# The first tile's pair weights of both expert calls added into cleared DRAM tables by GpSimd, one-hot products for the other dense tiles

## The chip, the cores and the metric

The kernel runs on one core of a Trainium2 chip. Its time is the device time of one execution in microseconds (us). Differences are told against the median of three runs of the kernel before, 3693.56 us (3688.54 to 3696.64).

## The reference

Two transformer-like blocks follow each other over a sequence of 256 rows, with 256 more rows of context in the first layer. Most of the time goes into the expert layers ("PEER") of the first block, and they are all that the change touches. For each row h and each of 8 heads, 16 of 16384 experts are chosen; an expert number is a pair (i, j) of keys of 0 to 127 each:

```python
def _peer(h, wq, keys, u, v):
    q = (hb @ wq).reshape(tc, PEER_HEADS, 2, PEER_HALF)
    s = jnp.einsum('thpk,hpnk->thpn', q, keys)
    s_top, i_top = lax.top_k(s, PEER_TOPK)
    cand = s_top[:, :, 0, :, None] + s_top[:, :, 1, None, :]
    cid = i_top[:, :, 0, :, None] * N_KEYS + i_top[:, :, 1, None, :]
    best, pos = lax.top_k(cand.reshape(tc, PEER_HEADS, -1), PEER_TOPK)
    eid = jnp.take_along_axis(cid.reshape(tc, PEER_HEADS, -1), pos, -1)
    g = jax.nn.softmax(best, -1)
    act = jax.nn.gelu(jnp.einsum('td,thed->the', hb, u[eid]), approximate=False)
    return jnp.einsum('the,thed->td', g * act, v[eid])
```

D_MODEL is 1024, N_KEYS 128, PEER_HEADS 8, PEER_TOPK 16: each row has 128 chosen pairs (i, j) with a share g each. The first layer has four tiles of 128 rows (two of the sequence, two of the context), the second layer two.

## The kernel before

**How an expert layer is computed.** A dense tile doesn't gather its experts. It goes through all of them in two halves. The *score half* has 128 rounds, one per key: a round takes 128 experts' u rows (512 KB; SyncE loads two rounds' worth as a unit of 1 MB into `expert_ring`, 4 slots), splits them into a high part (ScalarE, `expert_high`) and a low part (VectorE, `expert_ring_low`), and multiplies them in 24 products with the tiles' rows in high and low parts; the gelu of the result goes to DRAM or is kept. The *v half* has 128 rounds as well: gelu times the *pair weights* of that key is split and multiplied with the v rows.

**Pair weights** are a table of 128 x 128 numbers for each row t: at (i, j) stands the sum of the shares of row t's chosen pairs (i, j), and zero elsewhere; for the v half they are wanted with i on the partitions. Which pairs are chosen is worked out during the score half itself, by VectorE (`select`, a generator: VectorE runs its pieces beside the ring's low parts, so much a round as a budget in nanoseconds allows). For each dense tile the selection, three columns per pair (i, j, share), is transposed by TensorE and copied to `pair_table`. The one-hot tables are then made in *table groups* of TOKS = 4 rows: VectorE compares `iota` with the table (`equal`, one instruction of 128x1024), ScalarE scales one of the two sides by the shares, TensorE makes one product per row (one-hot of i by weighted one-hot of j) into PSUM, ScalarE takes it out.

**First expert call** (`first_experts`, classes `ExpertsVector`, `ExpertsTensor`, `ExpertsScalar`, `ExpertsSync`, `ExpertsPool`). Its tiles are selected in the order TILES = (0, 3, 1, 2); 0, 1 and 2 are dense (DT = 3, DW = 384 columns), 3 is SPARSE. Table groups start in round TABLES_AT = 32: 96 groups, one a round, two in the twelve even rounds of 60 to 82 (`DOUBLED`). Blocks of 16 rows of the tables are staged and stored to `w_dram` by SyncE (`store_w`), and read back in the v half (24 blocks, `load_w`). The v half's rounds have 18 products each. The sparse tile's 128 pairs per row are handled one by one, as 128 *picks*: GpSimd gathers a u row for each partition by indirect DMA (into 3 slots, named `x` in rows of the profile, U_SLOTS = 3), VectorE multiplies it with the tile's rows and sums (line 3027), gelu follows for 8 picks at a time, GpSimd gathers the v row (`chosen_v`, V_SLOTS = 4) and VectorE adds it, weighted (line 3048). From the end of the selection on, these picks fill VectorE's budget. The budgets are EARLY_NS 3900, TABLE_NS 3300, PICKS_NS 2200 in three parts of the score half and DOWN_NS 1450 in the v half. Modulation products of a later stage are laid into some of the score rounds (`mod_slot`, 12 units).

**Second expert call** (`peer_experts` with PT = 2 tiles, W = 256 columns): selection on VectorE with a budget of SELECT_NS = 1650 a round, GROUPS = W / TOKS = 64 table groups, one in each round from TABLE_AT = 128 - 64 = 64 on; the tables stay in SBUF (`wt`, named `expert_weights`). There are no sparse picks, and GpSimd does nothing here.

**Order.** Each engine runs its instructions in program order. SyncE issues all plain loads and stores, in order; a load behind a wait in its queue waits too. GpSimd issues the indirect DMAs. The stage before the first expert call (`mixer`, lines about 1688 to 1693 on SyncE) loads `ab_w_in`, the scan mask, and two sets of weights (`in_w_mod`, `in_ab_w_out`) through `weight_ring`.

Lines that the rows below name: 2925 and 1922 the low parts of a round in the first and the second call, 3058 the comparison of a table group, 3178 and 2088 one of three sets of products of a round in the first and the second call (eight products a round each), 3217 the products of the first call's v half, 1897 a reduction of the second call's selection (the last piece but one of a tile), 3001 the shares of a tile in the first call's selection, 1176 the scan that reads the mask, 1305 the modulation product of the mixer stage.

## Time and profile before

| | us |
|---|---|
| median of three runs | 3693.56 (3688.54 to 3696.64) |
| the profiled execution, its own time | 3688.0 |
| its span in the trace | 3686.2 |
| TensorE busy | 3516.4 (95%) |
| VectorE busy | 2731.1 (74%) |
| ScalarE busy | 1690.3 (46%) |
| GpSimd busy | 348.6 (9%) |
| first call: score half | 485.7 to 1175.6 |
| first call: v half | 1183.2 to 1713.4 |
| second call: score half | 2012.9 to 2443.1 |

The profile has names of its own for the engines: PE is TensorE, with PEld its weight loads, DVE VectorE, ACT ScalarE, POOL GpSimd, SP SyncE, and SPq a DMA on SyncE's queue. A row of a timeline begins with the start and the duration in us, then engine, line, operation, output and input, and in brackets the engine's idle time before it and what ended that. A row of a group has the count behind the x, then busy time in us, mean in ns of one, and idle time before them. A row of a table by stretches has the stretch in us from the span's start, its length, the busy time of TensorE and of its weight loads with counts in brackets (of the named line alone, where one is named; of all five engines where none is), the granted clock of TensorE as a share of the full one, the share of time in which the DMA engines were busy, and GB/s moved.

### The profile page before, as it was taken

How to read it: one execution, taken by the hardware profiler on the slowest of the kernel's cores; microseconds unless marked ns; L12 is line 12 of the kernel's file. 1: busy time of each engine (PE TensorE's matmuls, PEld its weight loads, DVE VectorE, ACT ScalarE, POOL GpSimd, SP SyncE). 2: the span in 40 equal slices, each digit the busy share in tenths (PEclk: the TensorE clock that was granted, in tenths of full speed). 3: DMA queues.
4: the chain of work that ended last, by engine and by line, in shares of the span. 5: the costliest groups of instructions: out<-in, count | busy, mean ns of one | idle time of the engine just before them, and what ended most of it. 6: DMA issues, size and time to landing. Idle time of an engine off the chain costs nothing. (4 is left out here: it accounts for less than half of the span.)

```text
span 3686.2 us, 56123 instructions
## 1 busy us (share of the span) xinstructions
PE 3516.4 (95%) x21807; PEld 3143.1 (85%) x21807; DVE 2731.1 (74%) x5467; ACT 1690.3 (46%) x3033; POOL 348.6 (9%) x274
## 2 busy tenths in 40 slices
PE   7999999989999999998999999999997899989899
PEld 6777998989998888887778999988886889988798
DVE  4557379988885888887546987778887677767775
ACT  4343333556663333334543444443334545564554
POOL 0000000014443333330000000000000000000000
PEclk9999999999999999999999999999998999999999
DMA  5133357569998999995124765556664214432143
GB/s 229 71 115 137 138 194 300 173 224 340 371 375 296 333 391 370 377 357 186 56 86 156 233 220 172 169 197 243 242 245 165 98 63 169 186 142 109 69 183 137
DMA packets 184072, 766.75 MB, mean 208 GB/s; under 512 B 23360, under 2 KB 70976, under 8 KB 133888
## 3 DMA queue, kind: packets, MB, share of 16 engines
q1 hardware_dynamic: 146944, 628.92, 47.3%
q0 software_dynamic: 36864, 134.23, 9.4%
q8 instruction: 175, 2.87, 0.3%
q14 instruction: 89, 0.73, 0.1%
HBM read 696.24 MB, written 66.85 MB: 207 GB/s over the span
## 5 line engine op out<-in xcount | busy, mean ns | idle before, releaser
L2925 DVE TENSOR_TENSOR expert_ring_low<-expert_ring,expert_high 128x1024 fp32r<-128x1024 f32 x256 | 312.9, 1222 | 143.5 <-ACT expert_high L3283 137.2
L3283 ACT ACTIVATE expert_high<-expert_ring 128x1024 fp32r<-128x1024 f32 x256 | 270.6, 1057 | 276.2 <-PE ps L3217 264.0
L2192 ACT ACTIVATE expert_high<-expert_ring 128x1024 fp32r<-128x1024 f32 x256 | 270.6, 1057 | 211.3 <-PE ps L2119 211.3
L1922 DVE TENSOR_TENSOR expert_ring_low<-expert_ring,expert_high 128x1024 fp32r<-128x1024 f32 x256 | 311.6, 1219 | 70.7 <-ACT expert_high L2192 70.7
L3178 PE MATMUL ps<-hidden_high,expert_high 128*128 128x384 f32 x1024 | 352.6, 344 | 0.0
L3179 PE MATMUL ps<-hidden_low,expert_high 128*128 128x384 f32 x1024 | 344.4, 336 | 0.0
L3180 PE MATMUL ps<-hidden_high,expert_ring_low 128*128 128x384 f32 x1024 | 344.0, 336 | 0.0
L2088 PE MATMUL ps<-peer_hT_high_peer,expert_high 128*128 128x256 f32 x1024 | 293.9, 287 | 0.6 <-DVE expert_ring_low L1922 0.5
L2089 PE MATMUL ps<-peer_hT_low,expert_high 128*128 128x256 f32 x1024 | 287.0, 280 | 0.0
L2090 PE MATMUL ps<-peer_hT_high_peer,expert_ring_low 128*128 128x256 f32 x1024 | 287.0, 280 | 0.0
L3484 POOL DMA_INDIRECT x<-in_peer_rows,spots x128 | 171.1, 1336 | 971.0 <-ACT mod_next L2378 558.8
L3217 PE MATMUL ps<-expert_high,weighted_high 128*128 128x512 f32 x768 | 237.7, 391 | 9.4 <-DVE weighted_low L3098 9.4
L3217 PE MATMUL ps<-expert_ring_low,weighted_high 128*128 128x512 f32 x768 | 237.0, 390 | 0.0
L3217 PE MATMUL ps<-expert_high,weighted_low 128*128 128x512 f32 x768 | 237.0, 390 | 0.0
L5596 PE MATMUL ps<-hT_high,units_high 128*128 128x256 f32 x704 | 200.2, 284 | 0.0
L5596 PE MATMUL ps<-hT_low,units_high 128*128 128x256 f32 x704 | 199.5, 283 | 0.0
L5596 PE MATMUL ps<-hT_high,weight_ring_low 128*128 128x256 f32 x704 | 199.4, 283 | 0.0
L3490 POOL DMA_INDIRECT chosen_v<-in_peer_v,spots x128 | 171.1, 1336 | 263.2 <-DVE x L3048 246.9
L2088 PEld LDWEIGHTS ps<-peer_hT_high_peer,expert_high 128*128 128x128 f32 x1024 | 194.4, 190 | 1.2 <-DVE expert_ring_low L1922 1.2
L219 DVE TENSOR_TENSOR weight_ring_low<-weight_ring,units_high 128x1024 fp32r<-128x1024 f32 (+1 forms) x148 | 166.9, 1189 | 38.3 <-ACT units_high L210 38.1
L3178 PEld LDWEIGHTS ps<-hidden_high,expert_high 128*128 128x128 f32 x1024 | 194.1, 190 | 0.8 <-issue 0.8
L2089 PEld LDWEIGHTS ps<-peer_hT_low,expert_high 128*128 128x128 f32 x1024 | 194.7, 190 | 0.0
(790 smaller groups left out, 9616.4 us busy)
## 6 DMA issues: line engine op xcount, KB each, us to landing
expert_ring<-in_peer_u SPq DMA_DIRECT2D x128, 1024.0 KB
expert_ring<-in_peer_v SPq DMA_DIRECT2D x128, 1024.0 KB
weight_ring<-in_ffn_w_up SPq DMA_DIRECT2D x22, 2048.0 KB, 7.3
weight_ring<-in_w_in SPq DMA_DIRECT2D x14, 2048.0 KB, 7.8
weight_ring<-in_w_mod SPq DMA_DIRECT2D x12, 2048.0 KB, 8.6
mod_slot<-in_w_mod SPq DMA_DIRECT2D x12, 2048.0 KB, 10.4
pair_weights<-pair_weights_out SPq DMA_DIRECT2D x24, 1024.0 KB
pair_weights_in<-pair_weights SPq DMA_DIRECT2D x15, 1536.0 KB, 15.6
```

What stands on the lines that cost most here:

```text
L1922: dve.tensor_tensor(piece(low, n), piece(raw, n), high[:, n % LEAD, :].bitcast(F32), ALU.subtract).then_inc(low_done, 1)
L2088: pe.matmul(o, b[:, s], hT_h[:, c, :], start=(c == 0), stop=False)
L2089: pe.matmul(o, b[:, s], hT_l[:, c, :], start=False, stop=False)
L2090: mm = pe.matmul(o, lo[:, s], hT_h[:, c, :], start=False, stop=(c == DC - 1))
L2192: act.activation(high[:, n % LEAD, :], piece(raw, n), ACT.Identity).then_inc(high_done, 1)
L2925: dve.tensor_tensor(self.piece(G.e_low, n), self.piece(G.e_raw, n), G.e_high[:, n % LEAD, :].bitcast(F32), ALU.subtract).then_inc(self.S.l ...
L3178: pe.matmul(o, b[:, s], B.hs[0][:, c, 0:DW], start=(c == 0), stop=False)
L3179: pe.matmul(o, b[:, s], B.hs[1][:, c, 0:DW], start=False, stop=False)
L3180: mm = pe.matmul(o, lo[:, s], B.hs[0][:, c, 0:DW], start=False, stop=(c == DC - 1))
L3217: mm = pe.matmul(G.ps[:, 2 * t + h, :], (B.ah, B.al)[x][:, r % 3, t * P:(t + 1) * P], v[y][:, h * 512:(h + 1) * 512], start=(r == 0 and (x ...
L3283: act.activation(G.e_high[:, n % LEAD, :], self.piece(G.e_raw, n), ACT.Identity).then_inc(S.high_done, 1)
L5596: mm = pe.matmul(G.ps[:, k % 8, 0:SEQ], w[x][:, c, q * P:(q + 1) * P], self.hT[y][:, c, :], start=(c == 0 and (x, y) == PASSES[0]), stop=( ...
```

## The change

*In both expert calls tile 0 (STREWN) leaves the one-hot path.* Its pair weights are made in DRAM: two areas, 8 blocks of `w_dram` (`pair_weights`) for the first call and `late_pairs` (`late_pair_weights`) for the second, are cleared in the mixer stage by 16 DMAs of 1 MB each from a constant of zeros. VectorE works out, for each partition (row) and pair, the place in that area (`own_spots`, `spots`), and GpSimd issues 128 indirect DMAs a call, each of which adds 128 shares, one per partition, to their places (`strew`; every sixteenth waits for all before it to land). The transposition and the table groups of that tile go: 64 groups are left in the first call, from round 48 (TABLES_AT) to 111, one each, and 32 in the second, from round 96. In the first call 96 strews stand ahead of the sparse tile's gathers on GpSimd, the other 32 between them. The second call loads tile 0's weights from `late_pairs` to SBUF in 9 DMAs, three in the score half and six in the v half. VectorE's budgets in the first call become 3200, 3000, 2300 and 1500.

```diff
@@ mixer stage, SyncE
                     ws.run_ahead(sp, u0 + 6)
+                    for b in range(OWN_BLOCKS):
+                        sp.dma_start(G.w_dram[b], G.d["zeros"]).then_inc(G.cleared, 16)
+                    for k in range(0, P, 2 * P // CLEARS):
+                        sp.dma_start(G.late_pairs[k:k + 2 * P // CLEARS, :].rearrange("i (p n) -> (i p) n", n=2 * D), G.d["zeros"]).then_inc(
+                            G.cleared, 16)
@@ peer_experts
-GROUPS = W // TOKS
+GROUPS = (W - P) // TOKS
+CLEARS = 16
+    LOADS = [(N_KEYS - KEPT, KEPT), (0, 12)] + [(k, 16) for k in range(12, N_KEYS - KEPT, 16)]
@@ peer_experts, VectorE
+                    if t == 0:
+                        step(dve.scalar_tensor_tensor(where[:, :], sel[:, t, 0, :], float(N_KEYS), sel[:, t, 1, :], ALU.mult,
+                                                      ALU.add))
...
+                    if t == 0:
+                        dve.wait_ge(base_landed, 16)
+                        dve.tensor_scalar(spots[:, :], where[:, :], float(P), base[:, 0:1], ALU.mult, ALU.add).then_inc(own_ready, 1)
@@ peer_experts, GpSimd
+        @block.gpsimd
+        def _(pool):
+            places = G.late_pairs.rearrange("i (n o) -> (i n) o", o=1)
+            pool.wait_ge(G.cleared, 16 * CLEARS)
+            pool.wait_ge(own_ready, 2)
+            for m in range(PAIRS):
+                if m and m % PEER_TOPK == 0:
+                    pool.wait_ge(G.strewn, 16 * (PAIRS + m))
+                pool.indirect_dma_start(places, bass.IndirectOffsetOnAxis(spots[:, m:m + 1], 0), shares[:, m:m + 1], None,
+                                        compute_op=ALU.add).then_inc(G.strewn, 16)
@@ peer_experts, SyncE
+            def load_pairs(n):
+                first, size = LOADS[n]
+                by_key = G.late_pairs.rearrange("i (j t) -> i j t", t=P)
+                sp.dma_start(wt[:, first:first + size, 0:P], by_key[:, first:first + size, :]).then_inc(pairs_landed[n], 16)
...
+                if p == UNITS_U - 3:
+                    sp.wait_ge(table_ready, 1)
+                    if mod is not None:
+                        sp.wait_ge(mod_out, 1)
+                    sp.wait_ge(G.strewn, 2 * 16 * PAIRS)
+                    for n in range(3):
+                        load_pairs(n)
...
+                if q % 8 == 0 and 3 + q // 8 < len(LOADS):
+                    load_pairs(3 + q // 8)
@@ first call
-TABLES_AT = 32
-TABLES = DW // TOKS
+TABLES_AT = 48
+TABLES = (DW - P) // TOKS
-EARLY_NS, TABLE_NS, PICKS_NS, DOWN_NS = 3900, 3300, 2200, 1450
+EARLY_NS, TABLE_NS, PICKS_NS, DOWN_NS = 3200, 3000, 2300, 1500
-DOUBLED = range(60, 84, 2)
-TABLE_ROUND = [r for r in range(TABLES_AT, N_KEYS) for _ in range(2 if r in DOUBLED else 1)][0:TABLES]
+STREWN = 0
+STREWN_FIRST = 6 * PEER_TOPK
+OWN_BLOCKS = P // BLOCK
+TABLE_ROUND = range(TABLES_AT, TABLES_AT + TABLES)
@@ first call, SyncE, before the loads for the v half
-                sp.wait_ge(S.table_ready, DT)
+                sp.wait_ge(S.table_ready, DT - 1)
+                sp.wait_ge(G.strewn, 16 * PAIRS)
@@ first call, GpSimd
+    def strew(self, pool, m):
+        G, B = self.G, self.B
+        places = G.w_dram.rearrange("b p (n o) -> (b p n) o", o=1)
+        if m and m % PEER_TOPK == 0:
+            pool.wait_ge(G.strewn, 16 * m)
+        pool.indirect_dma_start(places, bass.IndirectOffsetOnAxis(B.own_spots[:, m:m + 1], 0), B.own_share[:, m:m + 1],
+                                None, compute_op=ALU.add).then_inc(G.strewn, 16)
 
     def run(self, pool):
         G, S, B = self.G, self.S, self.B
+        pool.wait_ge(G.cleared, 16 * CLEARS)
+        pool.wait_ge(S.own_ready, 2)
+        for m in range(STREWN_FIRST):
+            self.strew(pool, m)
         pool.wait_ge(S.spots_ready, 1)
...
+            if STREWN_FIRST + n < PAIRS:
+                self.strew(pool, STREWN_FIRST + n)
```

**What stands on SyncE in the mixer stage**, between the last loads of `ab_w_in` and the two sets of weights that follow the mask; lines with + are new, lines with - are gone (the mask's load has another line number now).

```order
 L1688 DMA probs<-in_ab_norm_w 128x512
 L172 DMA weight_ring<-in_ab_w_in 128x4096 x3
-L1693 DMA scan_mask<-in_scan_mask 128x2560
+L1691 DMA pair_weights<-in_zeros 16x16384 x8
+L1693 DMA late_pair_weights<-in_zeros 16x16384 x8
+L1698 DMA scan_mask<-in_scan_mask 128x2560
 L172 DMA weight_ring<-in_w_mod 128x4096 x8
 L172 DMA weight_ring<-in_ab_w_out 128x4096 x2
```

Sixteen copies from DRAM to DRAM now stand ahead of the mask and of the weights behind it.

**What stands on GpSimd at the start of the first expert call**, before: `x` are the slots of the gathered u rows, `spots` the places of the sparse tile.

```order
L3601 UNCONDITIONAL_BRANCH
L3484 DMA x<-in_peer_rows,spots_4913 128x1024 x10
L3490 DMA chosen_v_4882<-in_peer_v,spots_4913 128x1024
L3484 DMA x<-in_peer_rows,spots_4913 128x1024
L3490 DMA chosen_v_4882<-in_peer_v,spots_4913 128x1024
```

And of the change, the last strews of the 96 and the first gathers: `big_21`, `big_44` and `big_34` are the waits for the sparse tile's places, for the last modulation unit and for the first table; `shares_strewn` counts strews that have landed.

```order
L3535 DMA pair_weights<-own_shares_4929,own_spots_4928 6291456x1 [waits shares_strewn]
L3535 DMA pair_weights<-own_shares_4929,own_spots_4928 6291456x1 x15
L3551 DMA x<-in_peer_rows,spots_4931 128x1024 [waits big_21,big_44,big_34]
L3535 DMA pair_weights<-own_shares_4929,own_spots_4928 6291456x1 [waits shares_strewn]
L3551 DMA x<-in_peer_rows,spots_4931 128x1024
L3535 DMA pair_weights<-own_shares_4929,own_spots_4928 6291456x1
```

The gathers that were first on GpSimd now stand behind 96 strews, and the first 32 of them have a strew between any two.

**What stands on SyncE where the second call goes from its score half to its v half**, before: `gelu_peer` is the store of a round's results, `big_15` the wait for the last table product.

```order
L2297 DMA gelu_peer<-gelu_out 128x512 [waits big_3]
L2280 DMA expert_ring<-in_peer_v 128x2048 [waits big_2] x2
L2287 DMA gelu_in_peer_20369<-gelu_peer 128x1024 [waits big_5,big_4] x2
L2308 DMA x<-x_spill 128x2048 [waits big_15]
L2280 DMA expert_ring<-in_peer_v 128x2048 [waits big_20] x4
```

And of the change:

```order
L2329 DMA gelu_peer<-gelu_out 128x512 [waits big_3]
L2311 DMA expert_weights<-late_pair_weights 128x4x128 [waits shares_strewn,big_13]
L2311 DMA expert_weights<-late_pair_weights 128x12x128
L2311 DMA expert_weights<-late_pair_weights 128x16x128
L2306 DMA expert_ring<-in_peer_v 128x2048 [waits big_2] x2
L2318 DMA gelu_in_peer_19921<-gelu_peer 128x1024 [waits big_5,big_4] x2
L2348 DMA x<-x_spill 128x2048 [waits shares_strewn,big_15]
L2306 DMA expert_ring<-in_peer_v 128x2048 [waits big_20]
```

Three loads of tile 0's weights, behind a wait for all strews, now stand ahead of the last two units of v rows (unit 66 and 67) that the score half loads.

## Rows read from the trace of the kernel before

**Rows 1.** The page's span, and its busy time by engine.

```profile
span 3686.2 us, 56123 instructions
PE 3516.4 (95%) x21807; PEld 3143.1 (85%) x21807; DVE 2731.1 (74%) x5467; ACT 1690.3 (46%) x3033; POOL 348.6 (9%) x274
```

**Rows 2.** Table by stretches, first call's score half, line 3178 alone.

```profile
485.70:654.50 168.80, 84.26 (x248) 46.58 (x248) 1.00 0.72 266
654.50:799.30 144.80, 72.50 (x209) 39.92 (x209) 0.98 0.53 179
799.30:826.80 27.50, 11.01 (x33) 6.05 (x33) 0.91 0.87 311
826.80:974.00 147.20, 70.08 (x201) 38.41 (x201) 0.98 0.94 343
974.00:1125.60 151.60, 82.66 (x241) 45.19 (x241) 1.00 0.98 375
1125.60:1175.60 50.00, 32.13 (x96) 17.97 (x96) 1.00 0.82 315
```

**Rows 3.** The same for the second call's score half, line 2088 alone.

```profile
2012.90:2178.60 165.70, 130.91 (x464) 88.02 (x465) 1.00 0.69 223
...
2204.60:2443.10 238.50, 142.39 (x489) 92.69 (x489) 1.00 0.52 171
```

**Rows 4.** Groups of VectorE in the first call's score half.

```profile
L2925 DVE TENSOR_TENSOR expert_ring_low<-expert_ring,expert_high 128x1024 fp32r<-128x1024 f32 x127 | 155.0, 1220 | 87.6 <-ACT expert_high L3283 82.8 <-issue 4.5
L3058 DVE TENSOR_TENSOR equal<-iota,pair_table 128x1024 f32<-128x1024 f32 x96 | 115.8, 1218 | 0.0
```

**Rows 5.** VectorE's timeline at four places.

```profile
493.64 1.23 DVE L2925 TENSOR_TENSOR expert_ring_low<-expert_ring,expert_high 128x1024 fp32r<-128x1024 f32 x1 [7.85 <-ACT expert_high L3283]
...
558.40 0.29 DVE L3001 TENSOR_TENSOR selected<-best_exp,best_sum 128x128 f32<-128x128 f32 x1
...
794.04 1.21 DVE L3027 SCALAR_TENSOR_TENSOR x<-x,hidden_rows 128x1024 f32<-128x1024 f32 x1
...
2091.72 2.27 DVE L1897 TENSOR_REDUCE selected<-one_hot 128x128 f32<-128x2048 f32 x1
```

**Rows 6.** Table by stretches, first call's v half, line 3217 alone.

```profile
1183.20:1713.40 530.20, 525.20 (x2304) 433.43 (x2304) 1.00 0.95 348
```

**Rows 7.** Timelines of GpSimd and VectorE around the first call's gathers.

```profile
657.35 1.39 POOL L3484 DMA_INDIRECT x<-in_peer_rows,spots  x1 [0.30 <-issue]
659.05 0.94 POOL L3484 DMA_INDIRECT x<-in_peer_rows,spots  x1 [0.30 <-issue]
...
803.89 1.89 POOL L3484 DMA_INDIRECT x<-in_peer_rows,spots  x1 [1.74 <-DVE x L3027]
...
816.65 1.22 DVE L3027 SCALAR_TENSOR_TENSOR x<-x,hidden_rows 128x1024 f32<-128x1024 f32 x1 [4.07 <-DMA x<-in_peer_rows,spots]
```

**Rows 8.** Groups of GpSimd, whole span.

```profile
L3484 POOL DMA_INDIRECT x<-in_peer_rows,spots x128 | 171.1, 1336 | 971.0 <-ACT mod_next L2378 558.8 <-DVE x L3027 400.2 <-issue 11.9
```

**Rows 9.** SyncE's timeline in the mixer stage.

```profile
112.11 0.33 SPq L172 DMA_DIRECT2D weight_ring<-in_ab_w_in  x1
115.16 0.33 SPq L1693 DMA_DIRECT2D scan_mask<-in_scan_mask  x1
152.68 133.08 SPq L172 DMA_DIRECT2D weight_ring<-in_w_mod  x8
```

**Rows 10.** Table by stretches, mixer stage, all engines.

```profile
112.00:153.00 41.00, 41.00 (x197) 28.97 (x195) 22.79 (x53) 17.43 (x36) 0.00 (x0) 1.00 0.21 84
153.00:196.00 43.00, 43.00 (x215) 30.57 (x215) 23.65 (x59) 18.20 (x42) 0.00 (x0) 1.00 0.13 50
```

**Rows 11.** Lines 1176 and 1305: ns min/median/max, first and last start.

```profile
L1176 DVE SCALAR_TENSOR_TENSOR mlstm_d<-ps,gcol,scan_mask x32: 475/617/753, 244.8 to 305.5; 128x256 f32<-128x256 f32 x16, 128x512 f32<-128x512 f32 x16
...
L1305 PE MATMUL ps<-weight_ring,silu_c x128: 592/592/617, 250.0 to 307.4; 128*32 128x512 f32 x128
```

**Rows 12.** The page's DMA issues: KB each, us from issue to landing.

```profile
pair_weights_in<-pair_weights SPq DMA_DIRECT2D x15, 1536.0 KB, 15.6
```

More of the change, by code:

```diff
@@ L97, in stage @@
         loads_landed = own[-1]
-        assert len(names) + (3 if beside is not None else 0) < len(own)
+        assert len(names) + (3 if beside is not None else 0) + (1 if loads else 0) <= len(own)
         @block.sync
@@ L1785, in peer_experts @@
         mod.slots = arena.take("mod_slots", [P, 2, UNIT], F32)
-    table, hot_i, hot_j, ge_in, aw, ah, al = small
+    spots, shares, base, table, hot_i, hot_j, ge_in, aw, ah, al = small
+    where = arena.take("spot_sums", [P, PAIRS], F32)
+    LOADS = [(N_KEYS - KEPT, KEPT), (0, 12)] + [(k, 16) for k in range(12, N_KEYS - KEPT, 16)]
     if end.cols:
@@ L1910, in select @@
+                    dve.tensor_tensor(share.rearrange("p (h m) -> p h m", h=PEER_HEADS), ex[:, t, :, :],
+                                      sm[:, t, :, 1:2].broadcast_to([P, PEER_HEADS, 16]), ALU.mult).then_inc((own_ready, sel_ready)[t], 1)
                     yield 300
-                for t in range(PT):
-                    at[f"turn{t}"] = at["now"] + TURN_AFTER
-                    yield (TURN_AFTER + 1) * SELECT_NS
-                    dve.wait_ge(sel_turned, t + 1)
-                    dve.tensor_copy(table[:, :, t * P:(t + 1) * P],
-                                    ps[:, 3, 0:3 * P].rearrange("p (k c) -> p k c", k=3)).then_inc(table_ready, 1)
-                    yield 600
@@ L1918, in select @@
-                assert at[f"turn{PT - 1}"] < TABLE_AT
+                at["turn"] = at["now"] + TURN_AFTER
+                yield (TURN_AFTER + 1) * SELECT_NS
+                dve.wait_ge(sel_turned, 1)
+                dve.tensor_copy(table[:, :, :], ps[:, 3, 0:3 * P].rearrange("p (k c) -> p k c", k=3)).then_inc(table_ready, 1)
+                yield 600
+                assert at["turn"] < TABLE_AT
             def split_low(n):
@@ L1940, in weigh @@
                     dve.wait_ge(ge_landed[m % 2], 16 * (m // 2 + 1))
+                for n, (first, size) in enumerate(LOADS):
+                    if expert(r) == first:
+                        dve.wait_ge(pairs_landed[n], 16)
                 if r >= 1:
@@ L2144, in _ @@
                     pe.wait_ge(score_s, SCORES // 2)
-                for t in range(PT):
-                    if r == at[f"turn{t}"]:
-                        turn_selected(t)
+                if r == at["turn"]:
+                    turn_selected()
                 u = mod_unit(r)
@@ L2216, in _ @@
                 split_high(r + LEAD)
-                if r == at["shift"]:
-                    for t in range(PT):
+                for t in range(PT):
+                    if r == at[f"shift{t}"]:
                         act.wait_ge(shift_ready, t + 1)
@@ L2997, in select @@
                 dve.tensor_copy(B.spots[:, :], B.where[:, :]).then_inc(S.spots_ready, 1)
+            elif tile == STREWN:
+                dve.wait_ge(S.base_landed, 16)
+                dve.tensor_scalar(B.own_spots[:, :], B.where[:, :], float(BLOCK), B.base[:, 0:1], ALU.mult,
+                                  ALU.add).then_inc(S.own_ready, 1)
             yield 600
             step.wait()
-            share = (B.share[:, :] if tile == SPARSE else sel[:, 2, :]).rearrange("p (h m) -> p h m", h=PEER_HEADS)
+            share = {SPARSE: B.share[:, :], STREWN: B.own_share[:, :]}.get(tile, sel[:, 2, :]).rearrange("p (h m) -> p h m", h=PEER_HEADS)
             mm = dve.tensor_tensor(share, B.ex[:, :, :], B.sm[:, :, 1:2].broadcast_to([P, PEER_HEADS, 16]), ALU.mult)
@@ L3003, in select @@
                 step(mm)
+                yield 300
+                continue
+            if tile == STREWN:
+                mm.then_inc(S.own_ready, 1)
                 yield 300
@@ L3184, in turn_selected @@
         G, S, B = self.G, self.S, self.B
-        k = [n for n, t in enumerate(TILES) if t != SPARSE][d]
+        k = [n for n, t in enumerate(TILES) if t not in (SPARSE, STREWN)][d]
         pe.wait_ge(S.sel_ready, d + 1)
@@ L3250, in run @@
                 pe.wait_ge(S.score_s, SCORE_GROUPS // 2)
-            for d in range(DT):
+            for d in range(DT - 1):
                 if r == at[f"turn{d}"]:
@@ L3421, in run @@
                     mod.load(sp, u + 2, self.mod_landed)
-            while stored < BLOCKS and TABLE_ROUND[4 * stored + 3] + 2 <= UJ * p + 1:
+            while stored < BLOCKS - OWN_BLOCKS and TABLE_ROUND[4 * stored + 3] + 2 <= UJ * p + 1:
                 self.store_w(sp, stored)
@@ L3582, in first_experts @@
     F.ln_cols = few.take("ln_cols", [P, 2, DC], F32)
+    B.base = few.take("own_base", [P, 1], F32)
     B.x_last = F.x_last = room(28.25, 4).take("x_last", [P, D], F32)
```

73 lines of the change are left out of this document (42 added, 31 removed).

## The prediction

> **What bounds the kernel now.** The page comes first: TensorE is busy 95% of a span of 3686.2 us [rows 1]. Its ends are modelled, so the share alone proves nothing; the rounds have to be timed. I cut both score halves (one round for each of 128 keys i) into stretches and counted rounds as eighths of the matmul records of one line [rows 2, 3].
>
> In the first call the 31 rounds from 485.7 take 168.8 us, 5.45 each; the next 26 take 144.8, 5.57 each; then 4 rounds take 27.5 and 25 take 147.2; the next 30 take 151.6, 5.05 each; the last 12 take 50.0, 4.17 each [rows 2]. The last ones hold no table group, the 30 before them one group each: 4.17 is TensorE's own pace for 24 products, and a table group (4 one-hot products) adds 0.88. In the second call 58 rounds without a group take 165.7 us, 2.86 each, and 61 of the 64 rounds with one take 238.5, 3.91 each: a group costs 1.05 [rows 3].
>
> Why the first call's rounds 31 to 56 are slower than 4.17 + 0.88 is read from VectorE. Each round it makes the low part of a key's rows and, from round 31, one comparison for a group; both are rows of 1.22 us [rows 4], and the rest of the round is selection. Selection runs from 493.64 to the first pick of the sparse tile at 794.04 [rows 5], 300.4 us with little idle time between. So the first call is VectorE's up to about round 57, and TensorE's behind it.
>
> The v halves are TensorE's: 2304 products in 530.2 us, at a DMA share of 0.95 [rows 6]. The change leaves their products alone.
>
> **Removed.** *Second call.* Tile 0 no longer passes through the table, so 32 of the 64 group rounds become plain: 32 x (3.91 - 2.86) = **33.6 us** on TensorE, whose rounds are back to back. VectorE needs 1.22 + 1.65 us in a plain round by its budget, which is the 2.86 measured, so selection hides as before.
>
> *First call*, in three pieces.
> (a) Rounds 0 to 30 hold no groups. TensorE's products, the modulation parts and kept rows set 168.8 us; VectorE's budget falls from 3.9 to 3.2 us a round, which nobody waits for here. Gain 0 (to 5).
> (b) Rounds 31 to 60 took 144.8 + 27.5 = 172.3 us. After, 13 of them hold a group: 30 x 4.17 + 13 x 0.88 = 136.5 us for TensorE. VectorE's check: selection now spreads over 61 of its rounds instead of 54 (+7 low parts of 1.2) with 16 comparisons in them instead of 25 (-9 x 1.2), so its work is some 298 us at most; rounds 0 to 60 last 168.8 + 136.5 = 305. It fits with little to spare; I take 138. Gain 34.
> (c) Rounds 61 to 115 took 147.2 + 151.6 = 298.8 us, twelve of them with two groups. After, rounds 61 to 111 hold one group and 112 to 115 none: 51 x 5.05 + 4 x 4.17 = 274.2. Gain 25. The last 12 stay at 50.0.
>
> The four rounds from 799.3 hold a stall that only moves: 27.5 - 4 x 5.05 = 7.3 us, where VectorE's first picks wait for rows [rows 2]. A gather issued at 803.89 is used at 816.65 [rows 7], 10.9 us after its issue ended. The next picks come in pairs per round while GpSimd now has a strew between any two gathers, so I charge 10 us for it after (7 to 16).
> First call: 34 + 25 - 10 = **49 us** gained.
>
> **Added, and what hides it.** *Strews.* A strew is an accumulating scatter of 128 four-byte words from GpSimd. None is in the trace. The nearest row is its indirect gather of 128 rows: 1.336 us mean, 0.30 us between two that wait for nothing [rows 7, 8], 1.64 us apiece. Below, 0.94 + 0.30 (the shortest shown); above, twice the work of a gather, as an add must read its target before it writes: 2 x 1.336 + 0.30 = 2.97. I take 1.64, the row itself. Every sixteenth waits for all before it to land: between 0 and 10.9 us; I take 4.
>
> First call: tile 0 is selected by round 14, so about 485.7 + 15 x 5.45 = 567, ready near 569 (before, at 558.4 [rows 5]). 96 strews: 157 us, 5 waits 20: GpSimd is free at **746**. Its first gathers must have landed for the first pick, behind round 61: 654.5 + 138 + 5 = about 798. Spare 50 us; the chain shows once a strew costs more than (798 - 569 - 20) / 96 = 2.18 us. The other 32 ride between picks: u, v and strew are 4.9 us of GpSimd, against a pick every 5.05 / 0.9 = 5.6 us. In this order the sparse gathers queue behind the strews on GpSimd, and VectorE, then TensorE, behind the gathers.
>
> Second call: tile 0's last reduction starts at 2091.72 [rows 5], ready near 2095. 128 strews 210 us, 7 waits 28: done at **2333**. SyncE waits for them behind round 123, at 2012.9 + 96 x 2.86 + 28 x 3.91 = 2397; what is queued behind that wait is every later load of expert rows. Spare 64 us; threshold 2.15 us a strew.
>
> *The rule that speaks against it.* GpSimd's row is of a gather that only copies [rows 8]. The Trainium skill (Collectives: The Full Stack, "The bandwidth ceiling: the fold count and why AG ≠ RS ≠ AR") says that a DMA which adds needs two source reads, so two read descriptors for each piece, and gets half a copy's rate. No run here shows one. By the rule the sum would be the first rival's, 3796; by the row it is 3614.
>
> *Clears.* 16 DMAs of 1 MB, DRAM to DRAM, on SyncE between the load at 112.11 and that of the mask at 115.16 [rows 9]. The core moves 84 GB/s in 112 to 153 and 50 in 153 to 196 [rows 10]; the mask is first read at 244.8, the weights loaded from 152.68 on at 250.0 [rows 9, 11]. What waits in SyncE's queue behind them is the mask and those weights, and VectorE's scan waits for the mask. 16.8 MB in 112.4 to 244.8, less 5 us for the mask, needs 132 GB/s. The trace has no DRAM-to-DRAM copy. Traffic ran at up to 375 GB/s [rows 2]; I take half of it as an estimate, since each byte is read from and written to DRAM: 188 GB/s, 90 us, over at 203. Cost 1 (0 to 5), issue included.
>
> *Pair loads of the second call.* Three of 2 MB together, in 512-byte pieces, go ahead of unit 66. The first call's load of the same pieces lands 1.5 MB in 15.6 us [rows 12]; 2 MB then take 21, and the first two (1 MB), which VectorE needs first, 10.4 of the 15.6 us of rounds 124 to 127. Unit 66 lands near 2422, needed near 2425. Cost 3 (0 to 8). The six later ones ride in a v half far from full.
>
> VectorE's share of v rounds grows by 50 ns of budget in 4.14 us. Nothing.
>
> **Sum**, against the profiled 3688.0: - 49 - 33.6 + 1 + 3 = -79, 3609. The median of the three runs is 5.6 above that execution, so 3693.6 - 79 = 3615; I say **3614**.
>
> **Rivals.**
> *1. A strew costs about twice a gather, and the result is slower.* At 2.97 us: first call 96 x (2.97 - 2.18) = 76 us before the first pick, second call 128 x (2.97 - 2.15) = 105 us of SyncE's wait. 3694 - 79 + 181 = **3796**. For it: the add's second read, and a landing of 10.9 us under load. Against: GpSimd's gathers vary from 0.94 to 1.89 us at one size [rows 7], so its time is not the bytes, and there are 128 words as there were rows. It decides from 2.52 us a strew on (224 c = 79 + 96 x 2.18 + 128 x 2.15). Chance 0.13.
> *2. The same, milder*: 2.2 to 2.5 us, at 2.35 a delay of 16 + 26: **3657**, still faster. 0.09.
> *3. VectorE stays the bound in the first call*, because selection in rounds 31 to 60 keeps its 5.57 us: 30 x 5.57 = 167, piece (b) gives 5 instead of 34: **3643**. Against it: its sum of work above. 0.08.
> *4. The clears are slow.* At 100 GB/s they end at 280 and the mask comes 40 us late: **3655**; at 81 GB/s they eat the gain. 0.03, and a third of that beyond.
> *Forecast* 0.67.
> In the first call's rounds 61 to 111 DMA is at a share of 0.98 and 375 GB/s [rows 2]; picks come 4.5% denser. If 375 were a wall, 0.04 MB more in 1.9 MB a round costs 51 x 0.11 + 2 = 8 us. It is in the range, not a rival.
>
> **Range.** The forecast's own bounds: (a) -5, stall -3 to +6, clears to +4, loads -3 to +5, DMA wall +8, DVE in (b) +6: 3600 to 3643, and to 3590 for what shorter strews and idle time might give. Rivals 3, 2 and half of 4 reach 3660. Low 3586, high 3662 leaves out rival 1 and some of the edges. A change within 0.2% (7 us) can't be told from none here: faster 0.85, same 0.02, slower 0.13.
>
> **What would show it.** In the trace after: second call, 96 rounds at 2.86 then 32 at 3.91, and no idle of TensorE from 2390 on for pair weights; first call, the first sparse pick at about 800 with GpSimd idle since 746; rounds with one group at 5.05; scan mask read without a wait for DMA. Wrong if a strew's row is above 2.1 us, if TensorE idles for a gather at the first pick, if the first v round of the second call starts more than 10 us after the last score round, or if the rounds 31 to 60 take over 150 us.

## The result, and the profile after

The changed kernel takes 3654.03 us (median of four runs, 3653.88 to 3655.86) against 3693.48 before: a ratio of 0.9896, 95% interval 0.9878 to 0.9913. It is faster by 39 us (32 to 45), where 79 were forecast: inside the stated range of times, but with a little under half of the forecast gain. Its profiled execution took 3654.15 us. Of the runs further down, two of the four executions of `plain_writes` and one of `strews_spread` fell in a slower state and are left out of their medians.

The page of the changed kernel, span and busy time by engine, as in [rows 1]:

```profile
span 3652.4 us, 54815 instructions
PE 3460.5 (95%) x21289; PEld 3086.7 (85%) x21289; DVE 2639.5 (72%) x5181; ACT 1623.9 (44%) x2843; POOL 830.3 (23%) x530
```

TensorE is busy 56 us less, the span is 34 us shorter: 22 us of new idle time have to be found. The stages, as in [rows 2, 3] (columns as there; line 3231 is a set of products of the first call's score rounds, 2105 of the second's):

```profile
489.50:658.00 168.50, 84.24 (x248) 46.55 (x249) 1.00 0.79 266
658.00:806.00 148.00, 82.38 (x241) 45.86 (x241) 0.98 0.62 161
806.00:1106.80 300.80, 152.88 (x441) 84.16 (x441) 0.98 0.97 351
...
1995.70:2273.00 277.30, 217.03 (x769) 145.85 (x769) 1.00 0.76 223
2278.00:2399.60 121.60, 72.33 (x248) 47.05 (x248) 1.00 0.64 154
```

The first three are the first call's rounds 0 to 30, 31 to 60 and 61 to 115: 168.8, 172.3 and 298.8 us before [rows 2]. The third was to fall to 284 and rose by 2. The last two are the second call's rounds 0 to 95 and 97 to 127.

The groups of GpSimd in the changed kernel (3535 the first call's *strews*, the indirect DMAs that add the shares; 2299 the second's; 3551 and 3557 the gathers of u and v rows):

```profile
L2299 POOL DMA_INDIRECT late_pair_weights<-pair_shares,pair_spots x128 | 246.8, 1928 | 488.5 <-DVE pair_shares L1924 412.9 <-issue 48.5 <-DMA late_pair_weights<-pair_shares,pair_spots 27.1
L3535 POOL DMA_INDIRECT pair_weights<-own_shares,own_spots x128 | 241.2, 1885 | 538.1 <-DVE own_shares L3050 473.6 <-issue 43.0 <-DMA pair_weights<-own_shares,own_spots 21.6
L3557 POOL DMA_INDIRECT chosen_v<-in_peer_v,spots x128 | 171.3, 1338 | 210.7 <-DVE x L3101 190.7 <-issue 20.1
L3551 POOL DMA_INDIRECT x<-in_peer_rows,spots x128 | 164.5, 1285 | 243.5 <-DVE x L3080 229.2 <-issue 14.3
```

A strew takes 1.885 and 1.928 us; with the idle time put down to issue (43.0 / 128 and 48.5 / 128) it is 2.22 us in the first call and 2.31 in the second, where the prediction took the gather's 1.64. The waits for landing, at seven places a call, are 21.6 / 7 = 3.1 and 27.1 / 7 = 3.9 us each; 4 was taken.

What that does in the first call, on GpSimd's and VectorE's timelines: the last of the 96 strews and the first gather, then a later stretch.

```profile
805.50 1.64 POOL L3535 DMA_INDIRECT pair_weights<-own_shares,own_spots  x1 [0.30 <-issue]
807.45 1.04 POOL L3551 DMA_INDIRECT x<-in_peer_rows,spots  x1 [0.30 <-issue]
808.87 2.46 POOL L3535 DMA_INDIRECT pair_weights<-own_shares,own_spots  x1 [0.38 <-issue]
...
843.33 1.23 DVE L3080 SCALAR_TENSOR_TENSOR x<-x,hidden_rows 128x1024 f32<-128x1024 f32 x1 [8.14 <-DMA x<-in_peer_rows,spots]
...
873.11 0.98 POOL L3551 DMA_INDIRECT x<-in_peer_rows,spots  x1 [0.31 <-issue]
874.39 1.76 POOL L3557 DMA_INDIRECT chosen_v<-in_peer_v,spots  x1 [0.30 <-issue]
876.45 1.61 POOL L3535 DMA_INDIRECT pair_weights<-own_shares,own_spots  x1 [0.30 <-issue]
878.37 1.33 POOL L3551 DMA_INDIRECT x<-in_peer_rows,spots  x1 [0.30 <-issue]
...
882.18 1.23 DVE L3080 SCALAR_TENSOR_TENSOR x<-x,hidden_rows 128x1024 f32<-128x1024 f32 x1 [3.34 <-DMA x<-in_peer_rows,spots]
```

GpSimd gets to its first gather at 807, not at 746. From there to the last strew its gaps are 0.3 us but for six (0.38 to 2.58 us, 9 us together): it is all but full while the strews ride between the gathers, and VectorE waits for rows, up to 8.14 us at a time. A table by stretches shows it for all engines (fifth pair: GpSimd):

```profile
848.00:976.00 128.00, 116.24 (x693) 114.38 (x694) 100.44 (x112) 70.99 (x164) 104.60 (x68) 0.95 0.96 332
976.00:1106.80 130.80, 130.80 (x822) 130.80 (x822) 114.59 (x125) 75.23 (x168) 70.52 (x50) 1.00 1.00 388
```

In the first stretch GpSimd issues 68 transfers in 128 us: 104.6 us of work and 67 gaps of at least 0.3 us leave some 3 us. TensorE idles 11.8 us there. The last strew goes out at 974; behind it TensorE has no idle time.

In the second call, SyncE and VectorE between the two halves:

```profile
2384.51 0.39 SPq L2329 DMA_DIRECT2D gelu_peer<-gelu_out  x1
2407.11 2.13 SPq L2311 DMA_DIRECT2D expert_weights<-late_pair_weights  x3
...
2410.33 0.42 DVE L1961 TENSOR_TENSOR weighted<-gelu_out,expert_weights 128x256 f32<-128x256 f32 x1 [10.18 <-DMA expert_weights<-late_pair_weights]
...
2411.59 1.22 PE L2134 MATMUL ps<-expert_high,weighted_high 128*128 128x512 f32 x2 [10.91 <-DVE weighted_low L1969]
```

The first strew of this call goes out at 2083.2 and the last ends at 2405.6: 322 us for the 128, where 238 were forecast. SyncE has waited 22 us for it, and TensorE 10.91 us.

And the clears, which cost nothing:

```profile
115.98 0.33 SPq L172 DMA_DIRECT2D weight_ring<-in_ab_w_in  x1
116.35 5.11 SPq L1691 DMA_DIRECT2D pair_weights<-in_zeros  x8
121.50 5.02 SPq L1693 DMA_DIRECT2D late_pair_weights<-in_zeros  x8
126.64 0.50 SPq L1698 DMA_DIRECT2D scan_mask<-in_scan_mask  x1
156.55 133.08 SPq L172 DMA_DIRECT2D weight_ring<-in_w_mod  x8
```

From the load ahead of them to the next weights it is 40.57 us, as before (112.11 to 152.68, [rows 9]). The 3.9 us by which all of this is late arise ahead of the clears, and at the first score product the changed kernel is still 3.8 us late (489.50 against 485.70), so nothing behind the clears waited for them. In the 41 us from 116 the core moves 355 GB/s against 84 before, in the next 43 us 181 against 50: that is 16.7 MB more, so by this table the 16.8 MB of zeros were over by about 200 at the latest, as forecast (203).

### The profile page after: what moved, and what is told of

It reads as the page before. It is cut to its first block and busy times, and to the rows that moved or that the text cites. A ratio compares the mean times of both kernels' runs of the same rounds, so it can differ in the third digit from the quotient of the medians.

```text
span 3652.4 us, 54815 instructions
## 1 busy us (share of the span) xinstructions
PE 3460.5 (95%) x21289; PEld 3086.7 (85%) x21289; DVE 2639.5 (72%) x5181; ACT 1623.9 (44%) x2843; POOL 830.3 (23%) x530
## 5 line engine op out<-in xcount | busy, mean ns | idle before, releaser
L3535 POOL DMA_INDIRECT pair_weights<-own_shares,own_spots x128 | 241.2, 1885 | 538.1 <-DVE own_shares L3050 473.6
L2299 POOL DMA_INDIRECT late_pair_weights<-pair_shares,pair_spots x128 | 246.8, 1928 | 488.5 <-DVE pair_shares L1924 412.9
```

## The experiments

Stages in us, each read from its own trace (first call's rounds 0 to 30, 31 to 60, 61 to 115; second call's rounds 0 to 95; from the last product of line 2105 in the second call to its first v product) and the median of the runs. The changed kernel's own two traces differ by 2.6 us in the rounds 61 to 115 and by 3.6 in the gap, so smaller differences than that say nothing. The profiled execution of `no_strews_1` was the fastest of its four (3626.0), that of `no_strews_2` the slowest (3656.3). The kernel before ran beside them at 3690.1, 3691.0 and 3691.5.

| kernel | 0-30 | 31-60 | 61-115 | second 0-95 | to v | median |
|---|---|---|---|---|---|---|
| before | 168.8 | 172.3 | 298.8 | 308.9 | 3.3 | 3693.5 |
| changed | 168.5 | 148.0 | 300.8 | 277.3 | 12.3 | 3654.0 |
| changed_again | 168.5 | 148.0 | 303.4 | 277.3 | 8.7 | 3655.4 |
| no_strews_1 | 168.5 | 147.9 | 281.3 | 277.3 | 8.2 | 3637.1 |
| no_strews_2 | 168.5 | 148.0 | 306.0 | 277.2 | 3.4 | 3647.1 |
| plain_writes | 284.0 | 146.6 | 288.7 | 337.6 | 3.4 | 3808.5 |
| gathers_ahead | 168.5 | 148.0 | 303.9 | 277.3 | 12.1 | 3656.2 |
| strews_spread | 168.5 | 148.0 | 287.7 | 277.3 | 8.4 | 3639.0 |
| budgets | 177.9 | 142.5 | 300.2 | 277.3 | 12.3 | 3655.8 |
| spread_and_budgets | 177.9 | 142.5 | 293.9 | 277.3 | 12.2 | 3652.9 |
| units_first | 168.5 | 147.9 | 303.7 | 277.3 | 9.9 | 3655.7 |
| second_call_only | 168.8 | 169.9 | 301.4 | 277.3 | 12.4 | 3672.5 |
| all_three | 168.5 | 148.0 | 284.1 | 277.3 | 12.2 | 3635.6 |

**No strews in the first call.** The other hunks only lower the counts that are waited for. Tile 0's pair weights of that call stay zero.

```diff
-        for m in range(STREWN_FIRST):
-            self.strew(pool, m)
...
-            if STREWN_FIRST + n < PAIRS:
-                self.strew(pool, STREWN_FIRST + n)
```

> The changed kernel without the 128 strews of the first call (left out: tile 0's pair weights of the first call, which stay zero); clears, budgets and table rounds as in the changed kernel. Theory G (GpSimd's strews, 2.2 us each and 2.4 with their waits, hold back the sparse gathers): the rounds 61 to 115 of the first score half come down from 300.8 us to about 282 (274 and the old stall of 7), and the whole to about 3636. Rival V (VectorE's own work, picks beside table groups, holds these rounds): no change, 3651 to 3656. By both the rounds 31 to 60 stay at about 148, since no gather is in them.

Measured 3637.07 us (ratio to before 0.986, 0.9844 to 0.9877), rounds 61 to 115 at 281.3 us, rounds 31 to 60 unchanged. Theory G holds in size, and V falls. Its groups of waits, VectorE between 795 and 1110 us:

```profile
DVE expert_ring_low L2972 <- ACT expert_high L3336: 27.0, 38, 2.0
DVE x L3080 <- DMA x<-in_peer_rows,spots: 13.0, 6, 5.6
```

In the changed kernel the second of these is 28.9 us with 8.6 more in two gaps put down to issue. This run also shows what the late first gather costs: here it goes out at 720, and VectorE's first pick still starts at 812.4, against 814.6 in the changed kernel, whose first score product is as much later (489.5 against 487.4). The end of the selection sets the first pick, not the gather; only from the second on, with its 6.51 us, does VectorE wait for rows in the changed kernel.

**No strews in the second call.** The counts waited for are lowered here too. Tile 0's pair weights of that call stay zero.

```diff
-            for m in range(PAIRS):
-                ...
-                pool.indirect_dma_start(places, bass.IndirectOffsetOnAxis(spots[:, m:m + 1], 0), shares[:, m:m + 1], None,
-                                        compute_op=ALU.add).then_inc(G.strewn, 16)
```

> The changed kernel without the 128 strews of the second call (left out: tile 0's pair weights of the second call, which stay zero); the pair loads stay. Theory G: SyncE's wait for the strews (22 us) goes, the gap of TensorE between score half and v half of the second call falls from 11.0 us to 2 to 4, and the whole to about 3643. Rival L (the three pair loads ahead of the last v units cost it, whenever they are issued): the gap stays near 11, the whole at 3651 to 3656.

The gap falls to 3.4 us, that of before (3.3). 3647.12 us (0.9879, 0.9862 to 0.9896). G holds: the strews' end is what TensorE waited for, the pair loads are not. The median falls by 6.9 us, the gap by 8.9. The v half of the profiled execution took 357.5 us against 354.0, but that execution was 9 us slower than the median of its kernel, so whether some of the gap goes back there isn't shown.

**Writes that don't add.**

```diff
-            pool.indirect_dma_start(places, ..., B.own_share[:, m:m + 1], None, compute_op=ALU.add)
+            pool.indirect_dma_start(places, ..., B.own_share[:, m:m + 1], None)
...                                              (the same in the second call)
```

> The changed kernel, its 256 strews as indirect writes that don't add (a pair chosen by two heads keeps one share only; otherwise the same). Theory A (an add costs a second read): the strew's row falls from 1.9 us to the gathers' 1.3, the waits for landing from 3.5 us to less, the first call gains some 17 us and the second some 10: 3627. Rival D (what costs is the issue of 128 pieces of 4 bytes on GpSimd, add or not): the rows stay at 1.9 us and the whole at 3651 to 3656.

GpSimd's groups of this kernel:

```profile
L2299 POOL DMA_INDIRECT late_pair_weights<-pair_shares,pair_spots x128 | 148.1, 1157 | 472.6 <-DVE pair_shares L1924 414.6 <-issue 39.3 <-DMA late_pair_weights<-pair_shares,pair_spots 18.8
L3534 POOL DMA_INDIRECT pair_weights<-own_shares,own_spots x128 | 137.9, 1077 | 522.0 <-DVE own_shares L3049 473.5 <-issue 36.9 <-DMA pair_weights<-own_shares,own_spots 11.5
```

And its table by stretches, all engines, while the first call's strews go out, with the changed kernel's two stretches behind:

```profile
600.00:650.00 50.00, 20.25 (x27) 5.26 (x28) 4.55 (x23) 1.43 (x2) 36.27 (x38) 0.50 0.12 30
650.00:700.00 50.00, 7.37 (x18) 5.16 (x18) 4.64 (x21) 1.43 (x2) 36.18 (x39) 0.50 0.02 0
...
600.00:650.00 50.00, 50.00 (x317) 43.26 (x317) 43.73 (x127) 18.11 (x25) 38.11 (x21) 1.00 0.94 305
650.00:700.00 50.00, 50.00 (x300) 48.31 (x299) 44.28 (x207) 18.42 (x26) 38.31 (x21) 1.00 0.66 166
```

Theory A is right on the row: without the add a strew takes 1.08 and 1.16 us in place of 1.89 and 1.93, and the wait for landing (11.5 + 18.8) / 14 = 2.2 us in place of 3.5. It was wrong on the time: the four executions took 3804.0, 3813.0, 3887.5 and 3895.2 us, and the faster two are 118 us slower than the kernel before. While GpSimd sends a DMA of 128 plain four-byte writes every 1.26 us, the core moves 30 and then 0 GB/s, where the changed kernel moves 305 and 166 in the same stretches; a unit of expert rows issued at 616 has the next one issued at 711, and TensorE all but stands still. The row says what an add costs on GpSimd, but not by its mean: VectorE stands still as well for much of this time (4.6 us of work in 50), and GpSimd's DMAs are shorter when it does. Of the strews that run beside no instruction of VectorE, those with the add take 1.57 us (10 in the first call) and 1.55 (3 in the second), those without it 0.96 (82 and 46): the add is worth 0.6 us. The gathers of the changed kernel take 0.95 to 0.98 so (17 of them). The whole says nothing on adds.

**First gathers earlier.**

```diff
-        for m in range(STREWN_FIRST):
+        for m in range(GATHER_AFTER):            # 5 * PEER_TOPK = 80
             self.strew(pool, m)
...
+        for n in range(U_SLOTS):
+            self.gather_u(pool, n)
+        for m in range(GATHER_AFTER, STREWN_FIRST):
+            self.strew(pool, m)
```

> The changed kernel, with the first three gathers of u rows (as many as there are slots) issued after 80 of the 96 leading strews, not after all of them. Theory G1 (it is the start of the picks that comes too late: VectorE waits 6.5 and 8.1 us for its second and sixth gather): the rounds 61 to 115 gain 6 to 12 us, 3642 to 3648. Rival G2 (GpSimd is full while strews ride between the picks, 5.4 to 6.9 us for u, v and strew against 5.6 us per pick): the wait comes back a few picks later, and the whole stays within 4 us of 3654.

3656.19 us (0.9917, 0.9899 to 0.9935), rounds 61 to 115 at 303.9. The whole came out as G2 says: VectorE's waits for rows move to later picks (41.7 us, 16 of them). Only the first three gathers are earlier here (768.5); the fourth still goes out behind the 96 strews, at 817.9. So this run alone doesn't rule out a late start; for the first pick `no_strews_1` does.

**Strews spread.**

```diff
-            if STREWN_FIRST + n < PAIRS:
-                self.strew(pool, STREWN_FIRST + n)
+            if n >= LAG - 1 and n % 3 != 2 and strewn < PAIRS:       # LAG = 10
+                self.strew(pool, strewn)
+                strewn += 1
```

> The changed kernel with its last 32 strews of the first call moved: none beside the first nine gathers of u rows, then two for every three picks, as far as pick 56. Theory G2 (GpSimd, with u, v and a strew to every pick, does 5.4 to 6.9 us of work per pick and VectorE waits for it): with 4.5 us of work per pick the rounds 61 to 115 come down from 300.8 us to 282 to 290, the whole to about 3640. Rival W (any strew in flight delays the landing of the gathers, wherever it stands): 298 to 303 us, the whole at 3651 to 3656.

Rounds 61 to 115 fall by 13.1 us to 287.7, with the same strews and the same adds. Three executions took 3626.1, 3639.0 and 3643.9 us (ratio 0.9849, 0.9818 to 0.9879; a fourth, of 14920 us, is not in the ratio). G2 holds and W falls: it is what GpSimd has to do per pick.

**VectorE's budgets.**

```diff
-            return EARLY_NS if r < TABLES_AT - 1 else TABLE_NS
+            return EARLY_NS if r < 31 else PLAIN_NS if r < TABLES_AT - 1 else TABLE_NS
-EARLY_NS, TABLE_NS, PICKS_NS, DOWN_NS = 3200, 3000, 2300, 1500
+EARLY_NS, PLAIN_NS, TABLE_NS, PICKS_NS, DOWN_NS = 4000, 2900, 2550, 2300, 1500
```

> The changed kernel with other budgets for VectorE in the first call: 4000 in rounds 0 to 30, 2900 in 31 to 46, 2550 from 47 on until the selection is done (before 3200, 3200 and 3000); strews as in the changed kernel. Theory V (in rounds 47 to 60 the low part, a comparison and 3.0 us of selection are 5.44 us of VectorE in rounds of 5.05, and ScalarE waits for the selection): rounds 31 to 60 fall from 148.0 to about 139; but the picks then start before GpSimd has got through its 96 strews, so the rounds 61 to 115 lose what was gained: sum of both at 445 to 449, the whole at 3650 to 3656. Rival P (those rounds are TensorE's and the 148 us are its own): 148 as before.

Rounds 31 to 60 fall to 142.5, so part of the 148 was VectorE's, as V says; but rounds 0 to 30 rise by 9.4 us to 177.9, which I had not expected. The trace of this run shows where, on ScalarE and TensorE (line 2408 is a modulation product, 3404 the exponentials of the selection):

```profile
665.60 0.31 ACT L3404 ACTIVATE best_exp<-best_shift 128x128 f32<-128x128 f32 x1 [7.57 <-DVE best_shift L3000]
...
666.45 1.86 PE L2408 MATMUL ps<-row_picker,mod_parts 128*128 128x2 f32 x8 [8.36 <-ACT mod_parts L2416]
```

ScalarE has reached the exponentials of the third tile selected before VectorE has their input. It waits 7.57 us, the modulation's parts stand behind that in its queue, and TensorE waits 8.36 us for them. Rounds 0 to 30 of the changed kernel have no idle time of TensorE. So this is theory V's wait again, in another place; that it took 168.8 us under the 3900 of before, where ScalarE also waited for the selection (5.8 us at the longest) but TensorE didn't, says that it hangs on what stands behind the wait. The sum of both stages, 442.7, is below the 445 to 449 expected; the whole is as it was (3655.75).

**Both**, with 88 strews ahead and the others five for every six picks.

> Both together, and 88 strews ahead of the gathers in place of 96, the other 40 five for every six picks from pick 9 on. Theories V and G2 together: rounds 31 to 60 at about 139 us and 61 to 115 at about 283, the whole at about 3628. If W holds: 139 and 300, 3645. If neither: 3654.

177.9, 142.5 and 293.9: each edit does what it did alone, the tighter spread less of it (GpSimd has 5 strews for 6 picks, not 4), and the whole is 3652.92. Of the 25 us that the forecast of 3628 missed, 9 are in the rounds 0 to 30, 11 in the rounds 61 to 115 and 3.5 in the rounds 31 to 60.

**V units ahead of the pair loads.**

```diff
-                if p == UNITS_U - 3:
+                if p == UNITS_U - 1:
                     sp.wait_ge(table_ready, 1)
```

> The changed kernel with the wait for the second call's strews and its three pair loads moved behind the last two v units on SyncE. Theory G (the strews' end at about 2407 sets the first v round; SyncE's order only adds to it): TensorE's gap between the halves stays at 11 to 13 us, the next rounds are up to 3 us faster, the whole 3650 to 3655. Rival S (the v units, held behind the wait, set the first v round): the gap falls to about 6 and the whole to about 3647.

A gap of 9.9 us and 3655.73 in all. The changed kernel itself shows 12.3 and 8.7 us in two traces, so this run decides nothing on the 2 us. A gap of 6 it was not: the last two v units were issued at 2391.2, 13 us before the pair loads (2404.1), and the first v product still started at 2408.5, behind the pair loads. Rival S falls.

**The second call alone.** The kernel before, with the hunks of `peer_experts` and eight clears.

> The kernel before with the change made in the second call alone (8 clears of 1 MB in the mixer stage; the first call as before). By the stages of the changed kernel's trace: score half 29 us less, the gap behind it 9 us more, its v half 2.5 us more: 16 to 20 us less than before, near 3673, and the first call's stages as before (172 and 299 us for rounds 31 to 60 and 61 to 115). Rival C (the clears or the two calls together cost what the stages don't show): gain under 12 us or over 24.

3672.49 us (0.9947, 0.9932 to 0.9962): 19 us less than before, in the 16 to 20 that the stages gave. The other half of the gain (3672.5 - 3655.4 = 17 us) is the first call's.

**Spread, gathers ahead and units first together.**

> The changed kernel with the last 32 strews spread as in the run with spread strews, the first three gathers ahead of the last 16 of the 96 strews, and the v units of the second call ahead of its pair loads. Theory G with both of its parts (once GpSimd keeps up with the picks, an earlier first gather does help): rounds 61 to 115 at 278 to 284 us in place of 287.7, the second call 2 to 3 us better: 3630 to 3636. Rival: the earlier gathers are worth nothing here either: 3637 to 3642.

3635.55 us (0.9849, 0.9835 to 0.9862), 20 us better than the changed kernel on the same chip; rounds 61 to 115 at 284.1, just outside what theory G gave, the whole at its upper end. The second call's gap did not move (12.2). Its ratio is that of the spread strews alone (0.9849), and 284.1 against 287.7 is hardly more than two traces of one kernel differ by, so that the earlier gathers add anything isn't shown. By its median it is the fastest complete version here.

**The changed kernel again.**

> The changed kernel as it is, beside the others on this chip: 3652 to 3657 by every theory; the stages 168.5, 148, 300.8 and 277.3 us (first call's rounds 0 to 30, 31 to 60, 61 to 115; second call's 0 to 95) within 1.5 us, the first v round of the second call 12 us behind the last score round; and by the view that the clears cost nothing, the same 40.6 us between the last load of the mixer's first weights and the first of the next, in which the clears stand.

3655.42 us. Three of the five stages agree to 0.1 us, rounds 61 to 115 were 303.4 (2.6 more, outside the 1.5 expected), the gap 8.7. The clears' stretch is again 40.56 us.

## What of the prediction held, and why it was wrong

**What held.** TensorE's pace: a table group is worth about what it was priced at. The second call's score half went from 432.7 us to 403.6, first to last product of line 2105 (2088 before): 29 of the 33.6 forecast. Piece (a), rounds 0 to 30: 168.5 us, no gain, as said. The clears: forecast 1, measured 0. The waits for landing: 4 taken, 3.1 and 3.9 measured.

**The step that failed** is "I take 1.64, the row itself". A strew is 2.22 and 2.31 us. The gather's row was the nearest one, but a gather only copies. Beside an idle VectorE a strew without the add costs what a gather does (0.96 against 0.95 to 0.98 us) and one with it 1.55 to 1.57: the 0.6 us between 1.64 and 2.22 are the add. The bound from above, 2.97 by two times the row, was too high; the truth lies in between, in the milder rival (2.2 to 2.5 us, 3657), which had 0.09. The Trainium skill's rule (Collectives: The Full Stack, "The bandwidth ceiling: the fold count and why AG ≠ RS ≠ AR"), that an adding DMA needs two source reads and gets half a copy's rate, was set aside for the row. It speaks of the rate of transfers; what these traces show is GpSimd's time for issuing one, which agrees with its direction, at 1.6 times (1.57 to 0.96) in place of 2.

From this one term follow three places:
- *Second call.* 128 strews end at 2405.6 where SyncE wanted them at 2384.5; TensorE waits 10.91 us. Forecast: 64 us to spare, no wait. Shown by no_strews_2: 12.3 to 3.4.
- *First call, the first pick.* "GpSimd is free at 746": it was 807. But this was cheap: the first pick started no later, counted from the first score product, than in no_strews_1, where its row was there long before, and gathers_ahead gains nothing.
- *First call, behind it.* "u, v and strew are 4.9 us of GpSimd, against a pick every 5.6": the sum is 1.29 + 1.34 + 1.89 + 3 x 0.3 = 5.4, before the waits for landing, and GpSimd was all but full from 848 to 976, 22 picks in 128 us, 5.8 us each. So for the first call the milder rival's mechanism (a late start) was not the one at work: the price was in the pace. That its 3657 came near the measured 3654 was luck. Shown from two sides: no_strews_1 takes off 19.5 us, strews_spread 13.1 with every strew left in. The charge of 10 us for the stall should have been 300.8 - 274.2 = 26.6, of which 281.3 - 274.2 = 7 are there without any strew.

How much of the miss this is, by the sum of stages below (33.5 us gained, 78.6 forecast, 45 missed): 16.6 in the rounds 61 to 115 and 6 in the gap of the second call (9.0, of which 3 were charged for the pair loads), 23 us in all. No run was made with the add at the price of a copy and all else equal, so this is a share by places.

**Mis-sized beside it: piece (b)**, rounds 31 to 60: 138 taken, 148.0 measured, 10 us of the miss. "It fits with little to spare" left out the budgets. Piece (a) notes that VectorE's falls to 3.2 us and that nobody waits for it there; but what VectorE may not do in the rounds 0 to 46 it has to do later. By the prediction's own numbers it may work 47 x (3.2 + 1.22) + 14 x (3.0 + 1.22 + 1.22) = 284 us until round 60, and the sum asked for up to 298. In the trace VectorE is busy 137.7 of the 168.5 us of rounds 0 to 30 (149.6 of 168.8 before), and the first pick starts at 814.6, not at 798. From round 47 on 5.44 us of VectorE stand against rounds of 5.05, it falls behind, and ScalarE, which does the exponentials of the selection between two splits of its own, waits for it:

```profile
778.20 0.31 ACT L3404 ACTIVATE best_exp<-best_shift 128x128 f32<-128x128 f32 x1 [5.14 <-DVE best_shift L3000]
...
782.17 2.05 PE L3256 MATMUL ps<-hot_weighted,equal 128*128 128x128 f32 x8 [4.61 <-ACT hot_weighted L3350]
```

TensorE idles 7.3 us in these rounds, 4.6 of them here, and its granted clock from 780 to 806 is 0.87. The run with other budgets took 5.5 of these 10 us back. Rival 3 (167 us) said the same much too strongly. The other 4.5 us stay open.

**Small terms that no row had asked for.** In the second call ScalarE now does the exponentials of each tile when its selection is ready, not both at once. ScalarE's timeline there:

```profile
2051.05 1.28 ACT L2235 ACT_TABLE_LOAD   x1
2054.30 0.31 ACT L2235 ACTIVATE best_exp<-best_shift 128x128 f32<-128x128 f32 x1 [1.96 <-DVE best_shift L1873]
2054.62 1.28 ACT L2213 ACT_TABLE_LOAD   x1
```

That is two loads of ScalarE's function tables (1.28 us each) and a wait once more than before, 4.8 us of ScalarE, and VectorE stood 2.2 us for the next high part; it fits the 277.3 us against 96 x 2.86 = 274.6. It was only read, not tested. The first v half took 534.5 us against 529.9 and the second 354.0 against 351.5; with the change in the second call alone the first stays at 529.3, so that part belongs to the first call's change (2 to 5 us in the traces that have it), by which step is open. The 3.8 us by which the first call starts later lie ahead of every instruction of the change (it is in the weight loads before 40 us) and are 1.7 to 4.8 us in the other traces.

**The sum**, in the two profiled executions: first call's rounds 22.7 less, second call's score half 29.1 less, its gap 9.0 more, the two v halves 4.6 and 2.5 more, start 3.8 more, between the calls 2.7 less, the rest 1.1 more: 33.5 of the 33.8 us by which the spans differ.

## What to carry to other kernels

When the trace has no row for an operation, the nearest row is only a price if the operation does the same; where a term of the work is new (here the add), take a value above the row, and look at what the forecast is worth there: between 1.64 and 2.3 us for one instruction this one lost some 23 of its 79 us. An engine that "has time" has to be checked for its pace against the consumer's, pick by pick, and not only for when it is done; spreading the same 32 instructions over more picks was worth 13 to 16 us, starting earlier nothing that shows. A budget per round is also a ceiling: work that it keeps out of the early rounds comes back in the late ones, and one that exceeds the round is a lag that some other engine's queue will wait for.

## What the runs showed of the hardware

- GpSimd's time for an indirect DMA of 128 pieces, with no instruction of VectorE beside it: 0.95 to 0.98 us for a gather of 4 KB rows, 0.96 for plain four-byte writes, 1.55 to 1.57 for four-byte writes that add. Long rows gathered and short words written cost the same; the add did not. With 0.3 us between two, a plain write goes out every 1.26 us.
- Such plain writes all but stopped the core's other traffic in the first call (30 and 0 GB/s in two stretches of 50 us, against 305 and 166 with adding ones at one every 2.2 us). In the second call they did so less: 131 to 202 GB/s from 2200 to 2400. Whether it is the pace, the kind of write or the place written to was not tried.
- GpSimd's time for one and the same adding DMA ranged from 1.54 to 4.18 us. In the first call the 54 strews above 1.63 us have instructions of VectorE with two tensor inputs beside them for 71% of their time, the 74 others for 30%; in the second call it is 43% (63 strews) and 34%. This is a reading of overlaps, not a test, and the second call bears it out only weakly. The Trainium skill (GPSIMD Engine Reference, "1. Specifications") names the SBUF interface that GpSimd shares with VectorE, with contention where VectorE has two SBUF inputs; the overlaps of the first call agree.
